# Hybrid encoder trunk: router products in column pairs, expert rows from the chosen experts alone, selection matrix released by blocks

## The reference

```python
x = x + (mixed @ w_out[l]).astype(x.dtype)
h = rms_norm(x, norm2_g[l])
x = x + hier_moe(h, ...)
...
g_logits = (hf @ w_rg + b_rg)
g_sel = jnp.argmax(g_logits, axis=-1)
e_logits = (hf @ w_re + b_re).reshape(T, N_EXPERT_GROUPS, EXPERTS_PER_GROUP)
top_val, top_idx = lax.top_k(e_logits[tok, g_sel], TOP_K_IN_GROUP)
gate = p_group[:, None] * jax.nn.softmax(top_val, axis=-1)
expert_id = g_sel[:, None] * EXPERTS_PER_GROUP + top_idx
...
ys = (jax.nn.silu(xb @ w_gate[e]) * (xb @ w_up[e])) @ w_down[e]
```

## Time and profile before

| | us |
|---|---|
| median of 3 runs | 1794.19 |
| lowest and highest | 1792.57 and 1795.06 |
| the profiled execution | 1790.18 |
| its span | 1788.2 |
| PE, DVE, ACT, POOL busy | 1648.9, 656.2, 418.6, 294.7 |
| mean granted clock of PE | 0.967 |

### The profile page before, as it was taken

The page is one execution under the profiler, slowest core; times in us unless marked ns, Lnnn a source line. Parts: engine busy times, 40 slices in busy tenths (PEclk is TensorE's granted clock), DMA queues, the critical chain, the costliest instruction groups (busy, mean ns, idle before and its releaser), DMA issues.

```text
span 1788.2 us, 20385 instructions
## 1 busy us (share of the span) xinstructions
PE 1648.9 (92%) x8412; PEld 867.3 (49%) x8412; DVE 656.2 (37%) x1024; ACT 418.6 (23%) x713; POOL 294.7 (16%) x374
## 2 busy tenths in 40 slices
PE   7989999969999999998898999999699999999985
PEld 4635566554444444443356546664444444444422
DVE  1785556461111111221328765564511111112114
ACT  3554451111111111110145446402011111111101
POOL 5910490000000000000268006700000000000003
PEclk9998899989999999999999998999799999999998
DMA  7000302428999999999940003034199999999996
GB/s 301 1 1 1 142 2 36 188 94 330 429 427 428 429 427 428 428 427 428 371 171 1 1 11 132 1 82 198 64 417 428 428 428 428 428 427 428 428 428 265
DMA packets 56865, 469.87 MB, mean 263 GB/s; under 512 B 17825, under 2 KB 17825, under 8 KB 30242
## 3 DMA queue, kind: packets, MB, share of 16 engines
q1 hardware_dynamic: 44866, 444.39, 59.6%
q10 hardware_dynamic: 9600, 15.74, 2.3%
q0 software_dynamic: 2304, 8.39, 1.3%
HBM read 447.52 MB, written 18.88 MB: 261 GB/s over the span
## 4 chain that ended last, share of the span: by engine, by line
PE 61%; DMA 26%; DVE 6%; ACT 4%; issue 2%; SPq 0%; POOL 0%; POOLq 0%; DVEq 0%
DMA ring<-wu 26%; PE bank L840 17%; PE bank L529 9%; PE bank L832 6%; PE bank L663 6%; PE bank L870 4%; PE bank L603 2%; PE bank L590 2%; PE bank L570 2%; PE bank L618 2%; DVE ring L1315 1%; PE bank L790 1%; PE bank L500 1%; PE bank L841 1%; PE bank L717 1%
## 5 line engine op out<-in xcount | busy, mean ns | idle before, releaser
L840 PE MATMUL bank<-ring,hbuf 128*64 128x512 f32 x1024 | 460.2, 603 | 37.7 <-DMA ring<-wu 36.3
L841 PE MATMUL bank<-ring,hbuf 128*64 128x512 f32 x1024 | 461.4, 604 | 0.0
L1705 DVE COPY raw<-bank 128x256 f32<-128x256 f32 x64 | 27.2, 425 | 770.8 <-PE bank L856 768.0
L840 PEld LDWEIGHTS bank<-ring,hbuf 128*64 128x64 f32 x1024 | 138.6, 139 | 328.5 <-issue 326.3
L832 PE MATMUL bank<-raw,hbuf 128*128 128x256 f32 x1024 | 240.9, 390 | 15.6 <-DVE raw L1663 15.6
L870 PE MATMUL bank<-ring,raw 128*64 128x512 f32 x512 | 233.4, 598 | 5.2 <-DVE raw L1705 4.1
L872 PE MATMUL bank<-ring,raw 128*64 128x512 f32 x512 | 233.4, 598 | 0.0
L529 PE MATMUL bank<-hbuf,ring 128*128 128x512 f32 x480 | 212.3, 599 | 5.2 <-ACT raw L978 5.2
L832 PEld LDWEIGHTS bank<-raw,hbuf 128*128 128x128 f32 x1024 | 193.0, 193 | 45.7 <-issue 17.4
L1947 POOL DMA_INDIRECT raw<-expert_rows,dest_i x8 | 8.0, 995 | 1213.6 <-DMA expert_rows<-raw 1211.8
L529 PEld LDWEIGHTS bank<-hbuf,ring 128*128 128x128 f32 x480 | 91.4, 192 | 117.2 <-issue 115.2
(11 more groups left out here) (336 smaller groups left out, 1926.5 us busy)
## 6 DMA issues: line engine op xcount, KB each, us to landing
ring<-wg SPq DMA_DIRECT2D x64, 2048.0 KB, 18.6
ring<-wu SPq DMA_DIRECT2D x64, 2048.0 KB, 22.9
ring<-wd SPq DMA_DIRECT2D x64, 2048.0 KB, 20.7
ring<-w_in SPq DMA_DIRECT2D x8, 2048.0 KB, 15.2
expert_rows<-raw ACTq DMA_DIRECT2D x120, 128.0 KB, 9.4
ring<-w_out SPq DMA_DIRECT2D x4, 2048.0 KB, 8.0
x<-x_in SPq DMA_DIRECT2D x4, 512.0 KB, 7.8
ring<-w_in SPq DMA_DIRECT2D x2, 1024.0 KB, 14.1
```

Source lines behind the costliest of these rows:

```text
L840: mm(pb[2 + par][0:CAP, :], tokens[:, k, :], W_gate[par][:, k, :], start=(k == 0), stop=(k == KT - 1))
L841: last = mm(pb[2 + par][CAP:P, :], tokens[:, k, :], W_up[par][:, k, :], start=(k == 0), stop=(k == KT - 1))
```

## The change

Router: the eight products go alternately to array columns 0 to 63 and 64 to 127 (weights widened from 36 to 64 columns, which read into the next tile's), so that even tiles' sums stand in PSUM rows 0 to 35 and odd tiles' in 64 to 99. ScalarE copies 128 rows. In place of a transpose, a product with a new constant, `fold`, turns and adds the two halves.

Rows: `first_of` keeps the two experts' numbers, and their first rows are computed from these between the last two rows of h. Positions from PSUM (now bank 7) are multiplied with both one-hot tiles in one operation and summed, which gives a token's two positions; adding the first row and 4096 (FAR) for positions from 64 on gives its row. The overflow rows are computed behind the first selection matrix, into `rel_far`.

Selection: for each block of tokens one comparison with a scalar per row, then one operation that compares with the second row and adds; the second raises `oh` once per block. For the first tiles PE waits for one block at a time, and else for all four. `pick_t` is gone.

```diff
@@ -55,6 +55,7 @@
...
 ROUND = 12582912.0
+FAR = 4096.0
 
@@ -116,6 +117,8 @@
...
         ident = cst("ident")
+        router_at = PACK["router_w"][0]
+        router_w = pk[:, router_at:router_at + KT * RW + HD - RW]
         h = hbuf[:, 0:4096].rearrange("p (b d) -> p b d", b=NB)
@@ -192,11 +195,11 @@
...
         rt = [qd[:, 160 * i:160 * i + 160] for i in range(12)]
-        rlT = raw[0:RW, 1024:1536]
+        rlT = raw[:, 1024:1536]
         pick = [raw[:, 1024 * i:1024 * i + 1024].rearrange("p (b s) -> p b s", b=NB) for i in range(2)]
-        pick_t = raw[:, 2048:3072].rearrange("p (b s) -> p b s", b=NB)
         slot_ids = raw[:, 7168:7168 + GC]
         pick_o, pick_ot = (raw[:, 6656 + 256 * i:6912 + 256 * i].rearrange("p (b s) -> p b s", b=NB) for i in range(2))
+        rel_at, rel_far = small[:, 16:24], small[:, 48:56]
         rel = [small[:, NB * i:NB * i + NB] for i in range(2)]
@@ -787,8 +790,9 @@
...
                 for k in range(KT):
-                    last = mm(pb[3][0:RW, P * b:P * b + P], pcol("router_w")[:, RW * k:RW * k + RW],
-                              hT[:, k, P * b:P * b + P], start=(k == 0), stop=(k == KT - 1))
+                    at = HD * (k % 2)
+                    last = mm(pb[3][at:at + HD, P * b:P * b + P], router_w[:, RW * k:RW * k + HD],
+                              hT[:, k, P * b:P * b + P], start=(k < 2), stop=(k >= KT - 2))
                 last.then_inc(s["rlT"], 1)
@@ -809,13 +813,13 @@
...
                 pe.wait_ge(s["rlT_e"], on("rlT_e") + b + 1)
-                last = tr(pb[2][:, HD * b:HD * b + RW], rlT[:, P * b:P * b + P], ident[0:RW, 0:RW])
+                last = mm(pb[2][:, HD * b:HD * b + RW], rlT[:, P * b:P * b + P], cst("fold"), start=True, stop=True)
             last.then_inc(s["rl"], 1)
...
             chosen = rt[8][:, 0:NB * NE].rearrange("p (b e) -> p b e", b=NB)
-            mm(pb[1][:, 0:P + NE], cst("before"), rt[8][:, 0:P + NE], start=True, stop=False)
+            mm(pb[7][:, 0:P + NE], cst("before"), rt[8][:, 0:P + NE], start=True, stop=False)
             for c in range(NB):
-                last = mm(pb[1][:, NE * (c + 1):P + NE].rearrange("p (b e) -> p b e", e=NE), cst("ones"),
+                last = mm(pb[7][:, NE * (c + 1):P + NE].rearrange("p (b e) -> p b e", e=NE), cst("ones"),
                           chosen[:, c, :][:, None, :].broadcast_to([P, NB - c, NE]), start=False, stop=(c == NB - 1))
@@ -823,12 +827,15 @@
...
                 group, part = divmod(n, GRP)
-                pe.wait_ge(s["oh"], group + 1)
+                if n:
+                    pe.wait_ge(s["oh"], NB * (group + 1))
                 if n >= 2:
...
                     for b in range(NB):
+                        if n == 0 and i == 0:
+                            pe.wait_ge(s["oh"], b + 1)
                         last = mm(pb[n % 2][:, GC * i:GC * i + GC], h[:, b, P * k:P * k + P], pick[group % 2][:, b, :],
@@ -1172,7 +1179,7 @@
...
                 act.wait_ge(s["rlT"], on("rlT") + b + 1)
-                A(rlT[:, P * b:P * b + P], pb[3][0:RW, P * b:P * b + P], ACT.Copy).then_inc(s["rlT_e"], 1)
+                A(rlT[:, P * b:P * b + P], pb[3][:, P * b:P * b + P], ACT.Copy).then_inc(s["rlT_e"], 1)
 
@@ -1602,70 +1609,64 @@
...
 
-            def first_of(hot, values, top, ids, n):
+            def first_of(hot, values, top, ids, n, first):
 
...
                 link(TT(hot, hot, per_block(ids, n), ALU.mult))
-                link(V.tensor_reduce(out=col[9], in_=hot, axis=AX.X, op=ALU.min))
-                link(TT(hot, per_block(ids, n), bc(col[9], n), ALU.is_equal))
+                link(V.tensor_reduce(out=first, in_=hot, axis=AX.X, op=ALU.min))
+                link(TT(hot, per_block(ids, n), bc(first, n), ALU.is_equal))
 
...
             TT(g_rel, g_log, bc(col[0], EG), ALU.subtract).then_inc(s["gs"], 1)
-            first_of(g_hot, g_log, col[0], cst("group_id"), EG)
+            first_of(g_hot, g_log, col[0], cst("group_id"), EG, col[9])
 
...
-            first_of(hot1, e_in, col[1], cst("expert_id"), NE)
+            first_of(hot1, e_in, col[1], cst("expert_id"), NE, col[7])
             link(STT(out=rt[7][:, 0:NB * NE], in0=rt[4][:, 0:NB * NE], scalar=-2.0 * NEG, in1=rt[3][:, 0:NB * NE],
...
             link(V.reduce_max(col[2], e_msk, AX.X))
-            first_of(hot2, e_msk, col[2], cst("expert_id"), NE)
+            first_of(hot2, e_msk, col[2], cst("expert_id"), NE, col[8])
             link(TT(chosen, hot1, hot2, ALU.add))
...
 
+            both = lambda i: qd[:, 160 * i:160 * i + 320].rearrange("p (j w) -> p j w", j=2)[:, :, 0:NB * NE]
+            by_block = lambda ap: ap.rearrange("p (j b) -> p j b", j=2)
+            hots, mine = both(4), both(6)
+            mine4 = mine.rearrange("p j (b e) -> p j b e", b=NB)
+            place, first_row, bump = rt[9][:, 20:28], rt[9][:, 28:36], rt[9][:, 40:48]
+            rel_all = small[:, 0:2 * NB]
             h_row(2)
+            link(TS(first_row, first_row, BIG, float(CAP), ALU.add, ALU.mult))
             h_row(3)
             dve.wait_ge(s["cnt"], on("cnt") + 1)
-            pos = pb[1][:, 0:NB * NE].rearrange("p (b e) -> p b e", b=NB)
-            cnt = pb[1][:, P:P + NE]
-            far, near, mine = v3(7, NE), v3(6, NE), v3(3, NE)
-            ext, run, base = rt[10][:, 32:64], rt[10][:, 64:96], rt[10][:, 96:128]
-            many = qd[:, 1760:1760 + 7 * NE].rearrange("p (e m) -> p e m", m=7)
-            TT(near, pos, per_block(cst("expert_row"), NE), ALU.add)
-            link(TT(many, cnt[:, :, None].broadcast_to([P, NE, 7]), cst("chunk_end")[:, None, :].broadcast_to([P, NE, 7]),
-                    ALU.is_gt))
-            link(V.tensor_reduce(out=ext, in_=many, axis=AX.X, op=ALU.add))
-            link(V.tensor_tensor_scan(out=run, data0=cst("ones")[:, 0:NE], data1=ext, initial=0.0,
-                                      op0=ALU.mult, op1=ALU.add))
-
-            link(TT(base, run, ext, ALU.subtract))
-            link(STT(out=base, in0=base, scalar=float(CAP), in1=cst("far_row"), op0=ALU.mult, op1=ALU.add))
-            link(STT(out=far, in0=pos, scalar=float(CAP), in1=per_block(base, NE), op0=ALU.is_ge, op1=ALU.mult))
-            link(TT(far, far, near, ALU.add))
-            for j, hot in enumerate((hot1, hot2)):
-                link(TT(mine, far, hot, ALU.mult))
-                link(V.tensor_reduce(out=col[5 + j], in_=mine, axis=AX.X, op=ALU.add))
-                ins = V.tensor_copy(rel[j], col[5 + j])
-            link(ins)
+            pos = pb[7][:, 0:NB * NE]
+            cnt = pb[7][:, P:P + NE]
+            link(TT(mine, pos[:, None, :].broadcast_to([P, 2, NB * NE]), hots, ALU.mult))
+            link(V.tensor_reduce(out=by_block(place), in_=mine4, axis=AX.X, op=ALU.add))
+            TS(bump, place, float(CAP), FAR, ALU.is_ge, ALU.mult)
+            link(TT(place, place, first_row, ALU.add))
+            link(TT(rel_all, place, bump, ALU.add))
 
...
                     dve.wait_ge(s["xp"], GRP * (group - 1))
-                slots = slot_ids[:, None, :].broadcast_to([P, NB, GC])
-                at = float(GC * group)
-                STT(out=pick[group % 2], in0=slots, scalar=at, in1=rel[0][:, :, None].broadcast_to([P, NB, GC]),
-                    op0=ALU.add, op1=ALU.is_equal)
-                link(STT(out=pick_t, in0=slots, scalar=at, in1=rel[1][:, :, None].broadcast_to([P, NB, GC]),
-                         op0=ALU.add, op1=ALU.is_equal))
-                TT(pick[group % 2], pick[group % 2], pick_t, ALU.add).then_inc(s["oh"], 1)
-                dve.wait_ge(s["oh"], group + 1)
+                if group:
+                    link(TS(rel_at, small[:, 0:2 * NB], -float(GC * group), None, ALU.add))
+                of = rel_at if group else small[:, 0:2 * NB]
+                for b in range(NB):
+                    ins = TS(pick[group % 2][:, b, :], slot_ids, of[:, b:b + 1], None, ALU.is_equal)
+                link(ins)
+                for b in range(NB):
+                    STT(out=pick[group % 2][:, b, :], in0=slot_ids, scalar=of[:, NB + b:NB + b + 1],
+                        in1=pick[group % 2][:, b, :], op0=ALU.is_equal, op1=ALU.add).then_inc(s["oh"], 1)
 
             selection(0)
-            link(TS(rt[9][:, 20:28], rt[9][:, 20:28], float(LATE * CAP), None, ALU.min))
-            V.tensor_copy(dest_i[:, :], rt[9][:, 20:28]).then_inc(s["dest"], 1)
+            link(TS(place, rel_all, float(LATE * CAP), None, ALU.min))
+            V.tensor_copy(dest_i[:, :], place).then_inc(s["dest"], 1)
 
@@ -1675,6 +1676,22 @@
...
             link(TT(gate_w[:, NB:2 * NB], gate_w[:, 0:NB], small[:, 32:36], ALU.mult))
+
+            ext, run, base = rt[10][:, 32:64], rt[10][:, 64:96], rt[10][:, 96:128]
+            many = qd[:, 1760:1760 + 7 * NE].rearrange("p (e m) -> p e m", m=7)
+            link(TT(many, cnt[:, :, None].broadcast_to([P, NE, 7]), cst("chunk_end")[:, None, :].broadcast_to([P, NE, 7]),
+                    ALU.is_gt))
```

(22 more changed lines are left out.)

## The result

| | before | changed |
|---|---|---|
| median, us | 1793.97 (4 runs) | 1779.58 (4 runs) |
| lowest to highest | 1792.57 to 1795.06 | 1774.71 to 1781.86 |
| ratio, 95% interval | | 0.9919 [0.9904, 0.9934] |
| profiled execution, its span | 1790.18, 1788.2 | 1774.71, 1772.8 |

The kernel became 14.4 us faster; forecast were 13.8. The profiled execution is the fastest of its four, so its traces say where the time went, and the ratio how much it was.

A forecast was written before the change was run, and what follows sets the result against it. The expert stage was taken as fixed work behind its first gate and up product, whether PE or DMA paces it. 2 x (2.43 + 2.55 + 1.96) - 0.08 = 13.8 us off 1794.19 gave 1780.4, range 1775.5 to 1787.

The forecast's parts named there:

- Part 1: Router products in pairs on PE: a block takes 1.06 us instead of 1.87, three on the path, saving 2.43 a layer.
- Router 3: Last router block, said to hide behind DVE's features and rows of h, PE ready some 0.5 us earlier than DVE.
- Part 2: Rows from the chosen experts alone, on DVE ahead of the selection matrix: saves 2.55 us a layer, bounds 2.2 and 2.8.
- part 3: Selection matrix by blocks, first comparison to first picking product: 1.81 us instead of 3.77, saving 1.96 a layer.
- The 0.08 for the larger table of constants: First load of constants: 36 more of 2752 columns add 0.08 us, once.
- The clock: PE's low clock at the picking parts, losing 1.7 and 3.2 us: left unchanged, -1.5 to +1.5 over both layers.
- Rival (c): Between counts and picks, PE's clock stays up or rises at once as its pause shrinks: 1775.5 us; chance 0.08.
- Rival (d): From router blocks to logits, half-used columns drop the clock to 1.2 GHz: slower, up to 1810 us; chance 0.02.

The follow-up runs named there:

- e7: The changed kernel with a copy and four dependent operations of 1024 elements on DVE ahead of the first selection matrix; 1788.44 us, ratio 0.9978 to the kernel before.
- e5: The changed kernel with every router block's sixteen records issued twice, in pairs; one run, 1781.73 us.
- e8: The changed kernel measured again, with nothing altered; ratio 0.9921 to the kernel before.
- e6: The changed kernel with seven spare products on PE ahead of the counts and four between counts and picks, results unused; 1771.51 us, ratio 0.9880.
- e9: The changed kernel with only the seven spare products ahead of the counts, none between counts and picks; ratio 0.9920 to the kernel before.
- the single release: The changed kernel, but PE waits for all four blocks of the selection matrix before its first picking product; ratio 0.9918 to the kernel before.

## Why the prediction was right

- **Bound.** The expert stage follows its first products: 493.05 and 493.22 us from reload to the next layer's projections in the profiled pair, and e7's delay arrives at the end. DMA stayed at about 430 GB/s.
- **Part 1** (2.43 a layer, measured 2.65). The block is 1.02 and not 1.06: 16 records take 0.88 (0.90 forecast), and the change of mode costs 0.14, where I had read 0.19 to 0.20 and put in 0.16. Three blocks make 2.55. The other 0.10 is the start of the logits, which I had taken for a tie between DVE and the turned products: before, it came 0.04 behind the end of the rows of h (369.61 against 367.09 + 2.48), now it overlaps them by 0.09.
- **Router 3** was hidden, but by less than I said: 0.5 us of slack was forecast, and PE was through at 365.50 + 1.08 = 366.58 against 366.73, 0.15. What the prediction left out was ScalarE: its squares, root and router 2's copy stand ahead of its half of the last features, so PE waits 0.99 for it ahead of router 3. With router 3 only 0.15 from the path, the cover was nearly used up; e5 shows that a longer router 3 does come out.
- **Part 2** (2.55, measured 6.59 - 4.01 = 2.58) and **part 3** (1.96, measured 1.96) came out as reckoned, from rows of other stages with the same or near shapes: 0.42 for a product and a sum of 256, combining operations 0.40 apart. The 1.96 is exact by some luck: the comparisons took 1.18 and not 1.22 until the first combining operation (the prediction's own numbers make 4 x 0.36 less 3 x 0.08 = 1.20), and from the end of that operation to PE it was about 0.15 and not 0.11.
- **Sum**: 2.65 + 2.58 + 1.96 = 7.19 a layer, 14.4 in all; 13.8 was forecast and 14.4 measured. The total's interval is 2.7 us wide to either side, so that it agrees to 0.6 us is in part luck; the sum of the parts is the stronger evidence. The 0.08 for the larger table of constants isn't to be read: its transfer took 6.42 before, 6.46 in the changed kernel and 6.86 in e8.
- **The clock** was left unchanged with -1.5 to +1.5. In the profiled pair the picking parts went from 15.52 + 17.00 to 15.72 + 15.47, 1.3 us less, which covers the 1.1 us by which that pair differs more (15.5) than the medians do (14.4). At full clock they take 14.05 (e6) and not 13.8, so the low clock had cost 1.5 and 2.95 us, and not 1.7 and 3.2. In the eight cases with 3.2 us of idleness ahead of the picks they took 15.45 to 15.99, in the ten with 4.4 us and more 15.52 to 17.00: the shorter wait may be worth another half microsecond a layer (means of 15.70 and 16.27), but these few differ in more than that wait, and no run tested it alone. Rival (c), that a pause of 3.3 us would let the clock stay, fell: it was already at 0.50 from the wait ahead. What a pause of 3.2 us does to a clock that is still at 1.00 no run shows; e9's pause was 4.30. Rival (d) fell in the window from 340 to 362: 1.00.
- Not settled: parts of 2 to 4 us in the total, part 3 and the single release among them, where the ratios' intervals are as wide as the parts; and what lets the clock rise earlier or later in one execution than in the next.

## What to carry to other kernels

When a stage is a fixed amount of work behind one starting point, count from that point back along the chain that sets it, take each operation's price from a row of the same shape elsewhere in the trace, and test by a delay put on that chain whether the end moves with it. Where the outputs need less than half of the array's columns (36 of 128 here), paired bursts of 16 records between full-width products saved nearly half their time (0.85 of 1.87 us), and releasing a matrix in the pieces in which it is built brought its reader forward by 1.18 us. Look at each engine that feeds the chain before calling the last step hidden.

## What the runs showed of the hardware

- Changing from full width to column halves and back cost TensorE 0.14 us in all, by the difference between blocks of 32 and of 16 records (e5).
- TensorE's clock fell to its 1.2 GHz level within a pause of 4.3 us (e9: 0.76 on average from 378.0 to 378.5, with TensorE idle until 378.6, and 0.50 from there to 381.5); with spare products in the waits, pauses of 0.60 us ahead of the counts and 0.79 us ahead of the picks left it at 2.4 GHz (e6). The loss cost the picking parts 1.4 to 2.95 us, and spare products into a free bank took it back without delaying the first pick (65.12 against 65.17 us after the mark).
- Cut into four, the comparisons over 1024 elements cost DVE no more (1.14 us against 1.22 for one, with the scalar per row in the place of a broadcast operand), the combining operations 1.67, against 1.22 for a comparison and 1.23 for a sum over all 1024.
